# Two heads at a time on TensorE in the first mixer's dilated attention, and gate units in four parts

## The reference, cut to what matters

```python
IN_WIDTHS = (DIL_WIDTH, DIL_WIDTH, DIL_WIDTH, SWA_Q_WIDTH, SWA_KV_WIDTH, SWA_KV_WIDTH, D_MODEL, D_MODEL)
DIL_PATTERNS = ((128, 1), (512, 4), (2048, 16))

def dilated_attention(q, k, v):
...
    for gi, (window, dil) in enumerate(DIL_PATTERNS):
        lo, hi = gi * DIL_HEADS_PER_GROUP, (gi + 1) * DIL_HEADS_PER_GROUP
...
        o, lse = banded_attention(to_streams(q), to_streams(k), to_streams(v),
                                  slopes[lo:hi], window // dil, dil)
...
    alpha = jax.nn.softmax(jnp.stack(lses, axis=2), axis=2)
    y = jnp.einsum('btgh,btghd->bthd', alpha.astype(q.dtype), jnp.stack(outs, axis=2))
```

## Time and profile before

| | us |
|---|---|
| median of three runs | 1798.34 (1798.18 to 1803.49) |
| profiled execution | 1793.65 |
| its span | 1791.8 |

### The profile page before, as it was taken

The page is one execution under the profiler, slowest core; times in us unless marked ns, Lnnn a source line. Parts: engine busy times, 40 slices in busy tenths (PEclk is TensorE's granted clock), DMA queues, the critical chain, the costliest instruction groups (busy, mean ns, idle before and its releaser), DMA issues.

```text
span 1791.8 us, 29597 instructions
## 1 busy us (share of the span) xinstructions
PE 1686.8 (94%) x11478; PEld 1499.8 (84%) x11478; DVE 1288.9 (72%) x1439; ACT 1026.5 (57%) x1127; POOL 63.9 (4%) x56
## 2 busy tenths in 40 slices
PE   8999989889999999999989879899999999799998
PEld 7998878878877666677758769799998999799997
DVE  6545688675589999999987867575555888575554
ACT  4333465454678999999977354354334484343432
POOL 0000000000000000000006400000000020000000
PEclk9999999989999999999999989999999999999999
DMA  9562114065799999999996424246554555255540
GB/s 324 186 188 72 48 60 157 8 269 201 246 369 418 418 419 419 420 420 419 420 397 228 144 95 142 78 158 208 177 180 133 169 192 189 71 166 187 187 140 24
DMA packets 194960, 391.74 MB, mean 219 GB/s; under 512 B 6960, under 2 KB 152112, under 8 KB 178480
## 3 DMA queue, kind: packets, MB, share of 16 engines
q1 hardware_dynamic: 193200, 383.89, 59.1%
q0 software_dynamic: 1664, 6.52, 1.0%
HBM read 379.77 MB, written 10.62 MB: 218 GB/s over the span
## 4 chain that ended last, share of the span: by engine, by line
PE 61%; DMA 15%; DVE 14%; issue 6%; ACT 3%; DVEq 0%; SPq 0%; POOL 0%; ACTq 0%; POOLq 0%
DMA raw<-w_e_up_dram 13%; PE ps L664 10%; PE ps L665 10%; PE ps L669 10%; DVE wlo L1901 6%; PE ps L1000 3%; PE ps L821 3%; PE ps L892 2%; PE ps L890 2%; PE ps L898 2%; PE ps L959 2%; PE ps L953 2%; PE ps L845 2%; PE ps L955 2%; ACT whi L1328 2%
## 5 line engine op out<-in xcount | busy, mean ns | idle before, releaser
L1901 DVE TENSOR_TENSOR wlo<-raw,whi 128x2048 fp32r<-128x2048 f32 (+3 forms) x358 | 813.7, 2282 | 226.0 <-ACT whi L1328 219.6
L1328 ACT ACTIVATE whi<-raw 128x2048 fp32r<-128x2048 f32 (+3 forms) x358 | 675.5, 1891 | 340.9 <-PE ps L669 196.5
L664 PE MATMUL ps<-xh,whi 128*128 128x256 f32 x800 | 200.8, 291 | 11.9 <-DVE xl L1914 10.8
L665 PE MATMUL ps<-xl,whi 128*128 128x256 f32 x800 | 198.0, 287 | 0.0
L664 PE MATMUL ps<-xb_h,whi 128*128 128x256 f32 x768 | 186.9, 284 | 5.2 <-DVE arena L1983 5.2
L665 PE MATMUL ps<-xb_l,whi 128*128 128x256 f32 x768 | 186.4, 284 | 0.0
L664 PEld LDWEIGHTS ps<-xh,whi 128*128 128x128 f32 x800 | 156.2, 195 | 13.9 <-issue 11.6
L953 PE MATMUL ps<-whi,xh 128*128 128x512 f32 x528 | 160.7, 397 | 0.0
L665 PEld LDWEIGHTS ps<-xl,whi 128*128 128x128 f32 x800 | 156.5, 196 | 0.2
L664 PEld LDWEIGHTS ps<-xb_h,whi 128*128 128x128 f32 x768 | 147.4, 192 | 5.6 <-DVE arena L1983 5.6
L959 PE MATMUL ps<-wlo,xh 128*128 128x512 f32 x528 | 143.8, 397 | 6.6 <-DVE wlo L1901 5.2
(11 more groups left out here) (429 smaller groups left out, 2883.7 us busy)
## 6 DMA issues: line engine op xcount, KB each, us to landing
raw<-w_e_gate_dram SPq DMA_DIRECT2D x64, 1024.0 KB, 10.7
raw<-w_e_up_dram SPq DMA_DIRECT2D x64, 1024.0 KB, 10.7
raw<-w_e_down_dram SPq DMA_DIRECT2D x64, 1024.0 KB, 10.7
raw<-ffn_w_gate_up_dram SPq DMA_DIRECT2D x44, 1024.0 KB, 5.1
raw<-w_in_dram SPq DMA_DIRECT2D x30, 1024.0 KB, 5.8
raw<-ffn_w_down_dram SPq DMA_DIRECT2D x22, 1024.0 KB, 4.9
raw<-xa_w_kv_dram SPq DMA_DIRECT2D x16, 1024.0 KB, 5.6
raw<-xa_w_q_dram SPq DMA_DIRECT2D x8, 1024.0 KB, 5.3
```

Of the source, the lines that this page charges most:

```text
L664: nc.tensor.matmul(o[b], wh, h, start=b == 0 and a == 0, stop=False, skip_group_check=True)
L665: nc.tensor.matmul(o[b], wh, l, start=False, stop=False, skip_group_check=True)
L1328: nc.scalar.activation(whi[u % HL][:, 0:n], raw[u % RAW][:, 0:n], ACT.Copy).then_inc(hi_ready, 1)
L1901: v.tensor_tensor(wlo[u % HL][:, 0:n], raw[u % RAW][:, 0:n], whi[u % HL][:, 0:n].bitcast(F32), ALU.subtract).then_inc(lo_ready, 1)
```

## The change

The dilated steps are put in another order: per pair of heads first both heads' tile 0, then both heads' tile 1. TensorE takes two steps at a time: `score_two` issues the six products of both heads by turns between the two halves of the array's rows, and `mix_two` issues both heads' mixes by turns between the two halves of its columns. VectorE and ScalarE still go step by step. The outputs of all dilated steps go to bank 4, and bank 5 takes the second head's wide scores. The third groups of both heads share bank 1, so the last product of a wide pair waits on the first (`third_scored`). ScalarE's transposed probabilities get four buffers in the dilated part. The gate units are computed in quarters, 12 products in every step, and ScalarE's part for them moves from a % 4 == 2 to a % 4 == 3.

```diff
         def score_bank(step, g):
 
+            if "head" in step:
+                bank, at = 0 if step["head"] == 0 else 5, g * T
+                if step["nk"] == P:
+                    bank, at = step["head"], g * P
+                elif g == 2:
+                    bank, at = 1, step["head"] * T
+                return ps[:, bank, at:at + step["nk"]]
...
+        def mixed_bank(step, y):
+
+            return ps[:, 4 if "head" in step else 4 + (y + step.get("flip", 0)) % 2, :]
...
+        def turned_free(s, step):
+
+            if "head" in step:
+                return s - 3
+            return s - 3 if s in (2 * DIL_HEADS, 2 * DIL_HEADS + 1) else s - 1
...
-                for hh in range(DIL_HEADS):
-                    lo = HD * (hh % 2)
-                    for qt in range(2):
+                for pair, qt, head in product(range(DIL_HEADS // 2), range(2), range(2)):
+                        hh, lo = 2 * pair + head, HD * head
...
-        PT_first = [x[:, 3 * b:3 * b + 3, :].rearrange("p c (b q) -> p (c b) q", q=P) for b in range(2)]
+        PT_first = [v.rearrange("p c (b q) -> p (c b) q", q=P)
+                    for v in (x[:, 0:3, :], x[:, 3:6, :], sg[:, 8:11, :], sg[:, 11:14, :])]
...
+            def fourth_unit(u, part):
+
+                _, kc, n = units[u]
+                if part == 0:
+                    st["bank"] = lin_bank()
+                    weights_in(u)
+                b, ks = part // 2, range(part % 2 * kc // 2, (part % 2 + 1) * kc // 2)
...
+            def score_two(s, first, second):
+
+                if s >= 1:
+                    pe.wait_ge(att_biased, s)
+                turns = ((0, 2), (1, 0), (0, 0), (1, 1), (0, 1), (1, 2))
+                wide = first["nk"] > P
+                for n, (a, g) in enumerate(turns):
+                    step = (first, second)[a]
+                    q, k = step["scores"][g][0]
+                    if n == 5 and wide:
+                        pe.wait_ge(third_scored, st["third"])
+                    mm = nc.tensor.matmul(score_bank(step, g), q, k, start=True, stop=True)
+                    if n == 0 and wide:
+                        st["third"] += 1
+                        mm.then_inc(third_scored, 1)
+                mm.then_inc(att_scored, 2)
+
+            def mix_two(s, first, second, PT):
+
+                y = st["y"]
+                pe.wait_ge(att_pt, s + 2)
+                if y >= 1:
+                    pe.wait_ge(att_out, y)
+                at, per = first["qt"] * P, first["nk"] // P
+                n = len(first["pv"][0][2])
+                for a in range(n):
+                    for b, step in enumerate((first, second)):
+                        lo, _, pv = step["pv"][0]
+                        v, g, kt = pv[a]
+                        mm = nc.tensor.matmul(mixed_bank(step, y)[lo:lo + HD, at:at + P], v,
+                                              turned_in(PT, s + b, step)[:, g * per + kt, :], start=a == 0,
+                                              stop=a == n - 1)
+                        if a == n - 1:
+                            mm.then_inc(att_mixed, 1)
...
                 for a, step in enumerate(steps):
                     s = base + a
                     if between:
                         between(a)
-                    if a + 2 < len(steps):
+                    if two(a + 2):
+                        if a % 2 == 0:
+                            score_two(s + 2, steps[a + 2], steps[a + 3])
+                    elif a + 2 < len(steps):
                         score(s + 2, steps[a + 2])
                     turn(s, step)
-                    if a >= 1:
+                    if a >= 1 and two(a - 1):
+                        if a % 2 == 0:
+                            mix_two(s - 2, steps[a - 2], steps[a - 1], PT)
+                    elif a >= 1:
                         mix(s - 1, steps[a - 1], PT)
...
             def gates_between(a):
-                if a % 2 == 0:
-                    feature_unit(u_in[23 + a // 4], half=a % 4 // 2)
+                fourth_unit(u_in[23 + a // 4], a % 4)
...
-                if a % 4 == 2:
+                if a % 4 == 3:
                     u = u_in[23 + k]
                     ahead(u)
                     evac(u, st["lin"], sg[:, 2 * k:2 * k + 2, :])
```

More of the change, by code:

```diff
@@ L14 @@
 from contextlib import ExitStack
+from itertools import product
 import numpy as np
@@ L415, in attention @@
                         steps.append(dict(nk=nk, qt=qt, scores=sc, bias=bi, merged=True, sink=None, scale=0.125,
-                                          pv=[(lo, 0, pv)], last=hh % 2 == 1 and qt == 1,
+                                          head=head, pv=[(lo, 0, pv)], last=hh % 2 == 1 and qt == 1,
                                           y=[qd[:, hh // 2, :]]))
@@ L643, in _ @@
         def _(pe):
-            st = dict(lin=0, sq=0, step=0, xl=0, y=0, fresh=False)
+            st = dict(lin=0, sq=0, step=0, xl=0, y=0, fresh=False, third=0)
             def high_in(u, i=None, step=6):
@@ L717, in feature_unit @@
                 if half == 1:
+                    mm.then_inc(unit_used, 1)
+            def fourth_unit(u, part):
[4 more added lines that the diff above has]
+                b, ks = part // 2, range(part % 2 * kc // 2, (part % 2 + 1) * kc // 2)
+                wh, wl = wview(whi, u, kc, n), wview(wlo, u, kc, n)
+                mm = triple(st["bank"][:, b, :], [(wh[:, k, b * P:b * P + P], wl[:, k, b * P:b * P + P], xh[:, k, :],
+                                                   xl[:, k, :]) for k in ks],
+                            first=part % 2 == 0, last=part % 2 == 1)
+                if part == 3:
                     mm.then_inc(unit_used, 1)
@@ L822, in score @@
                 mm.then_inc(att_scored, 1)
+            def score_two(s, first, second):
[29 more added lines that the diff above has]
+                            mm.then_inc(att_mixed, 1)
+                if second["last"]:
+                    st["y"] += 1
             def turn(s, step):
@@ L844, in mix @@
                         w = v.shape[1]
-                        mm = nc.tensor.matmul(ps[lo:lo + w, 4 + y % 2, k * T + step["qt"] * P:k * T + step["qt"] * P + P],
-                                              v, PT[s % 2][:, g * per + kt, :], start=a == 0, stop=a == len(pv) - 1)
+                        at = k * T + step["qt"] * P
+                        mm = nc.tensor.matmul(mixed_bank(step, y)[lo:lo + w, at:at + P], v,
+                                              turned_in(PT, s, step)[:, g * per + kt, :], start=a == 0,
+                                              stop=a == len(pv) - 1)
                 mm.then_inc(att_mixed, 1)
@@ L852, in attend, with two @@
                 base = st["step"]
-                score(base, steps[0])
-                score(base + 1, steps[1])
+                def two(a):
+                    return a < len(steps) and "head" in steps[a]
+                if two(0):
+                    score_two(base, steps[0], steps[1])
+                else:
+                    score(base, steps[0])
+                    score(base + 1, steps[1])
                 for a, step in enumerate(steps):
```

19 lines of the change are left out of this document (12 added, 7 removed).

## The result

| | us |
|---|---|
| before, median of 12 runs | 1798.99 |
| after, median of 12 runs | 1804.64 |
| ratio | 1.0031, 95% interval 1.0021 to 1.0041 |
| profiled execution of after, its span | 1804.87, 1803.0 |

The changed kernel is 5.6 us slower. The forecast was 1800.6 in a range of 1790 to 1808. The time lies in the range, just past the 0.3% beyond which a difference counts, on the side that I had given 0.21. Of the runs told here three, one of before at 1873.19, one of the kernel with the high part back at 2337.52 and one with quarters in the dilated part only at 2508.16, lie far above the rest of their kernel at a lower clock, and the ratios leave them out.

The account below looks back on a forecast made before the run. TensorE was taken to bound the dilated part, a chain changing engines the windowed part. Stage end 1.2 us later, one clock fall 1.7 and opening -0.65 gave +2.2 on the median: 1800.6, range 1790 to 1808.

Parts of the forecast that it names:

- rival A: Attention stage: most of TensorE's eight pauses bring a clock fall; 6.3 us slower with three, 9.7 with five; chance 0.20.
- the opening: Start of the dilated part: first transposes at 159.2 instead of 162.1; clock back sooner, 0 to -1.3 us, half taken.
- Part 1: Dilated scores and mixes on TensorE: a pair's scores cost one head's, mixes 0.80 and 1.45; 4.6 us less per four steps.
- The new wait inside a wide pair: TensorE's wide dilated scores: waiting on the pair's own first product costs 0 us, at most 0.2 each, 0.8 in all.
- Rival C: Dilated pairs: paired products don't overlap in longer rows, giving 1804 to 1812 us; chance 0.07.
- Part 2: Gate units on TensorE: quarters of 1.63 us, four costing 6.52 against 6.14, 0.38 more per four steps.
- Part 3: ScalarE's moved high part makes VectorE's low part wait in the same step; dilated cycle 16.3 us, from 17.9.
- Rival B: VectorE's low part doesn't wait for the high part; dilated cycle 13.7, windowed about 14.5, total 1785 us; chance 0.13.
- Step 16: Start of the windowed part: its transposes at 224.3 instead of 230.96, a lead of 6.7 us.
- The clock: TensorE, dilated and windowed parts: eight pauses left, one clock fall taken, +1.7 us.
- the 0.6 that I had taken off: Windowed part: the same addition over the groups of before ends 0.6 us late, so that was subtracted from the stage end.

Follow-up runs that it names:

- the kernel with the high part back: Changed kernel with ScalarE's high part issued one step earlier again, at a % 4 == 2; quarters, pairs and evacuation stay: ratio 0.9915, median 1787.81 us.
- quarters in the dilated part only: Changed kernel with ScalarE's high part at a % 4 == 2 and gate units in halves in the windowed steps: ratio 0.9904, median 1783.92 us.
- The kernel with the low part later: Changed kernel with VectorE's low part one step later, the last in step 31; ScalarE's high part stays: ratio 0.9937, median 1788.62 us.
- the filled kernel: Changed kernel with 18 extra, never-read products before TensorE's transposes of steps 4, 8, ... 28: ratio 1.0009, median 1801.43 us.
- quarters alone: Kernel before with gate units in quarters and ScalarE's part moved to a % 4 == 3, heads one by one: ratio 1.0146, median 1826.9 us.

## Why the prediction was right or wrong

**The range and the sum.** The time, +5.6 on the median, lies in the range. The likeliest value, +2.2, was 3.4 too low. The case that came is rival A's, most pauses bringing a fall: seven lengths of lower clock where I had taken one. By A's own sum that is 1.2 + 7 x 1.7, 13.1, and outside my range. That the time stayed inside is partly luck: a fall cost 1.3 and not 1.7, the opening came earlier, and the medians differ by less than the stage.

**Part 1, pairs: right.** Twelve score records took 0.87 and 1.50 (forecast 0.86 and 1.49), mixes 0.81 and 1.46 (0.80 and 1.45). The new wait inside a wide pair costs 0, as taken; with it the pair took 1.50. Pairs alone gave 12 us. Rival C, pairs that don't overlap, falls. The run with one head after the other shows, however, that I had been right for less than I thought: I had taken the overlap of windowed groups over to longer ones, and it carries over only in the order by turns, which the change happens to have.

**Part 2, quarters: the hand-over was mis-sized.** I priced each quarter and each set of transposes with a hand-over of its own (1.63, 0.48, 0.80). The chain shows transposes between two quarters in 0.33 and 0.67 (176.06, 181.93); between scores and a mix they took 0.48 and 0.86 (169.63, 175.81 with the high part back). A quarter behind a mix took 1.61 to 1.63, one behind transposes 1.42 (176.39 to 177.82). Transposes and quarters use the whole array; the extra 0.15 to 0.2 stands in these rows only where halves of the array come in or go out. So TensorE's work per group is 13.05 (the kernel with the high part back), not 13.7, and the loop 15.8, not 16.3.

**Part 3, the moved high part: right, and it decides.** VectorE's idle time before the low part was forecast at some 3.3 and was 3.0 to 3.1 in the dilated groups and 3.5 at the end. Two opposite repairs, one on either engine, both remove it in every group where they part the two steps, and both make the kernel faster than before (1787.81 and 1788.62). Rival B, that the wait is not there, falls; the gain that it described is real and is what the repaired kernels have. Step by step, by the last transposes: the opening 157.2 for a forecast of 159.2; the first two groups 15.5, 16.1 for 15.8, 16.3; and with the pauses filled 15.9, 16.4, 16.6 for 16.3, 16.7, 16.5. (The 16.1 holds some 0.2 of the fall that begins at its end; from first transpose to first transpose the loop is 15.8. The forecast's 159.2 meant the first transpose, which came at 156.9. In the sum below the two cancel.) Step 16 came at 223.7, forecast 224.3; this closeness is luck, as two falls that were not forecast there, 1.9, stand against the early opening.

**The opening: earlier than forecast, by the clock.** I took half of a possible 1.3 us for a clock that is back sooner. In the changed kernel's trace the clock does not fall there at all (before: 0.50 from 156 to 160), and the first transposes come 5.2 earlier instead of 2.9. In the other traces a fall at 151 to 153 is there in some and missing in others, with equal code up to that point, so this is no effect that I can put down to the change. The kernel with the low part later, the same up to there, has a fall of 6.8 us at 151.1 and its first transposes at 159.1, as forecast; the changed kernel has none and 156.9. So the order of steps gave what was forecast of it, and the rest is a fall that was missing in this one trace. The -0.65 of the sum, half of 1.3, has no support as an effect of the change.

**The clock: the step that failed.** I counted eight pauses of TensorE, took one fall, 1.7, and gave three or more 0.20. Seven came, one of double length, six of them ahead of 265 us. They lie at the pauses. TensorE's records in order (in brackets the idle time before) show the first without a fall and the first three with one, at 188.2, 205.2 and 222.3:

```profile
172.44 0.55 PE L905 MATMUL ps<-c,scr 128*128 128x128 f32 x3 [2.76 <-DVE scr L2177]
...
188.27 0.90 PE L905 MATMUL ps<-c,scr 128*128 128x128 f32 x3 [2.77 <-DVE scr L2177]
...
205.66 0.69 PE L905 MATMUL ps<-c,scr 128*128 128x128 f32 x2 [2.77 <-DVE scr L2177]
...
223.42 0.47 PE L905 MATMUL ps<-c,scr 128*128 128x128 f32 x1 [4.02 <-DVE scr L2185]
```

Three pauses of 2.76 or 2.77 us: none, then a fall, then a fall. The groups that hold falls are longer than forecast by 1.0 and 0.9 (third and fourth), 2.5 (fifth), 3.1 (sixth, two falls) and 1.4 (seventh), 8.9 in all for seven lengths of 3.4 us, 1.3 for each; the filled kernel says 1.2. So the price was a little too high and the number far too low. The filled kernel shows cause and price in one: the same loop, the same wait on VectorE, TensorE's pauses of 2.8 to 4.0 us gone or cut to at most 2.0, one fall up to 265 us. What had kept me from rival A was a single place, 350 to 358 at a clock of 1.00. TensorE's records there show one pause as long as these:

```profile
356.32 0.88 PE L1142 MATMUL ps<-c,arena 128*128 128x128 f32 x6 [2.74 <-ACT arena L1696]
```

The row was true and is like the pause before 172.44, but its stretch ended too soon: two shorter pauses follow, 0.79 and 1.08 us, and at 361.38 the clock fell for 10.2 us, which a stretch up to 372 would have shown. The step that failed is to let one such place speak for eight. The Trainium skill, "TensorE: Matmul & The Clock Gate", section on HAM oscillation, says that repeated waits between bursts bring the lower clock back; the trace agrees in kind. By the rule alone every pause would have cost; the one before 172.44 didn't, nor did pauses of 2.3 (at 210.8 with the high part back), 2.4 (at 202.0 and 222.7 with quarters alone) and 2.05 (at 240.9 with the low part later). From 160 to 300 us the traces of all nine kernels hold 28 pauses of at least 1.97 us, and 23 have a fall that begins within 1.7 us of their end.

**How the sum closes.** The stage ends 7.8 late where 1.2 + 1.7 - 0.65 was forecast, a difference of 5.6. The clock makes 8.9 - 1.7 = 7.2 of it, the opening -2.0 + 0.65 = -1.35, the first two groups -0.3 and -0.2, the last -0.3 (13.7 for 14.0), and the 0.6 that I had taken off for the error of my addition, which this time was not there, +0.6: 5.65.

**What stays open.** Why of pauses of the same length some bring a fall and some don't was seen and not explained; what was tested is that falls go when the pauses are filled (seven to two ahead of 300 us) or broken up (quarters to halves in the windowed part, three to none ahead of 264, and one at 265.0). The 7.8 us of the stage and the 5.6 of the medians differ by 2.2, which one profiled execution of each kernel can't settle.

## What to carry to other kernels

When a step is moved on one engine, look up who consumes it under the same step number: two engines that handle the same item in the same step, where they had been a step apart, close a loop through every engine between them, and here that turned a gain of 12 to 15 us into a loss of 6. When the two are parted again, look also at what the later one now stands in front of: here one repair gave groups of 13.0 and the other 15.3. Count the single pauses that a change leaves on TensorE, and price each as likely to bring a fall, whatever one quiet place in the trace shows; 4.8 us of idle time in short pieces had no such price. Issue the products for the two halves of the array by turns.

## What the hardware showed that I had not expected

- Whether two halves of TensorE's array overlap depends on the order of issue: 24 records in 1.46 us by turns, 2.38 head after head; 12 in 0.81 and 1.07; wide scores 1.50 and 2.03.
- Between two kinds of work that both use the whole array there is no hand-over to pay (three transposes between two groups of full-array products 0.33, between scores and a mix on halves of the array 0.48).
- Products that nobody needs shortened the stage: with 18 of them ahead of each of seven sets of transposes the last low part starts at 282.74 instead of 290.10. The medians, 1801.43 and 1804.64, point the same way and are not clear of noise.
- Single pauses of TensorE of 2.0 us already had falls behind them, and two of seven pauses of 1.6 to 1.7 us, while 4.8 us of idle time in eight waits of at most 0.8 us had none.
- A later stage that no experiment touches differs too: near 340 to 400 us the lower clock lasted 10.2 us in the traces before and after, and 17.1 in one piece in every variant of the experiments, those that won time and the one that lost 26 us alike. So it doesn't follow the time won; what sets it is open.
